# The seam ahead of ret-out, and the first expert's context products

## The reference

```python
y_ret = (jax.nn.silu(g_ret) * o) @ w_ret_o              # o: retention output, normalised per head
y_conv = (cb * u) @ w_conv_o
merged = jax.nn.sigmoid(ga) * y_ret + jax.nn.sigmoid(gb) * y_conv
x = x + g1 * rmsnorm(merged @ w_o)

aff = jax.nn.softmax(hf @ w_router, axis=-1)            # hf: the modulated tokens
vals, idx = lax.top_k(aff.T, cap)                       # cap: 128 for latents, 16 for context
xs = hf[idx]
hid = jax.nn.silu(einsum('ecd,edf->ecf', xs, w_gate)) * einsum('ecd,edf->ecf', xs, w_up)
out = einsum('ecf,efd->ecd', hid, w_down) * vals[..., None]
y = zeros.at[idx].add(out)
```

## Time and profile before

| | us |
|---|---|
| median of 3 runs | 2106.55 |
| lowest, highest | 2105.34, 2106.89 |
| the profiled execution, its time | 2105.37 |
| its span in the profile | 2103.70 |
| PE busy in the span | 1996.7 (95%) |
| DVE busy | 1183.3 (56%) |
| ACT busy | 743.5 (35%) |
| POOL busy | 235.1 (11%) |

### The profile page before, as it was taken

The page is one execution under the profiler, slowest core; times in us unless marked ns, Lnnn a source line. Parts: engine busy times, 40 slices in busy tenths (PEclk is TensorE's granted clock), DMA queues, the critical chain, the costliest instruction groups (busy, mean ns, idle before and its releaser), DMA issues.

```text
span 2103.7 us, 32724 instructions
## 1 busy us (share of the span) xinstructions
PE 1996.7 (95%) x12747; PEld 1727.3 (82%) x12747; DVE 1183.3 (56%) x1623; ACT 743.5 (35%) x840; POOL 235.1 (11%) x241
## 2 busy tenths in 40 slices
PE   6999999989999999999999995799999999999992
PEld 3898988879999999999999884577777777777772
DVE  5654646465554232332122556777777777777765
ACT  7622121231111111111112332455556555556552
POOL 1010101000000000000000123111221111121102
PEclk9999999999999999999999997899999999999996
DMA  9011102224443111112224747388887788888668
GB/s 335 20 46 46 54 32 76 77 60 143 142 139 116 41 34 46 40 50 74 85 85 135 274 145 316 111 322 320 320 308 290 271 321 320 320 308 309 264 254 311
DMA packets 179510, 365.96 MB, mean 174 GB/s; under 512 B 10500, under 2 KB 99532, under 8 KB 178564
## 3 DMA queue, kind: packets, MB, share of 16 engines
q1 hardware_dynamic: 162736, 311.23, 40.6%
q0 software_dynamic: 16624, 54.04, 8.4%
q10 hardware_dynamic: 100, 0.03, 0.0%
HBM read 322.24 MB, written 43.02 MB: 174 GB/s over the span
## 4 chain that ended last, share of the span: by engine, by line
PE 90%; DVE 4%; DMA 4%; issue 1%; SPq 1%; ACT 1%; DVEq 0%; ACTq 0%
PE ps L912 10%; PE ps L913 10%; PE ps L914 10%; PE ps L1175 8%; PE ps L1177 8%; PE ps L1184 8%; PE ps L1193 8%; PE ps L934 3%; PE ps L935 3%; PE ps L936 3%; PE ps L983 2%; PE ps L985 2%; PE ps L984 2%; PE ps L1093 2%; PE ps L1095 1%; PE ps L1094 1%
## 5 line engine op out<-in xcount | busy, mean ns | idle before, releaser
L2080 DVE TENSOR_TENSOR e_lo<-raw,e_hi 128x2048 fp32r<-128x2048 f32 x192 | 439.3, 2290 | 92.8 <-ACT e_hi L1552 92.8
L1552 ACT CAST e_hi<-raw 128x2048 fp32r<-128x2048 f32 x192 | 367.1, 1914 | 213.5 <-PE ps L1184 213.5
L912 PE MATMUL ps<-h_hi,w_hi 128*128 128x384 f32 x960 | 322.1, 335 | 1.0 <-DVE w_lo L1662 1.0
L913 PE MATMUL ps<-h_lo,w_hi 128*128 128x384 f32 x960 | 321.1, 334 | 0.0
L914 PE MATMUL ps<-h_hi,w_lo 128*128 128x384 f32 x960 | 321.0, 334 | 0.0
L1662 DVE TENSOR_TENSOR w_lo<-w_raw,w_hi 128x1024 fp32r<-128x1024 f32 x64 | 78.0, 1219 | 215.3 <-ACT w_hi L1290 215.2
L912 PEld LDWEIGHTS ps<-h_hi,w_hi 128*128 128x128 f32 x960 | 180.6, 188 | 8.9 <-DVE w_lo L1662 4.6
L913 PEld LDWEIGHTS ps<-h_lo,w_hi 128*128 128x128 f32 x960 | 180.5, 188 | 0.0
L914 PEld LDWEIGHTS ps<-h_hi,w_lo 128*128 128x128 f32 x960 | 180.5, 188 | 0.0
L1175 PE MATMUL ps<-e_hi,x_hi 128*128 128x512 f32 x512 | 159.6, 393 | 0.2 <-ACT x_hi L1558 0.2
L1177 PE MATMUL ps<-e_lo,x_hi 128*128 128x512 f32 x512 | 157.7, 389 | 0.0
(11 more groups left out here) (281 smaller groups left out, 3275.6 us busy)
## 6 DMA issues: line engine op xcount, KB each, us to landing
raw<-in_w_gate_dram SPq DMA_DIRECT2D x64, 1024.0 KB, 7.8
raw<-in_w_up_dram SPq DMA_DIRECT2D x64, 1024.0 KB, 14.4
raw<-in_w_down_dram SPq DMA_DIRECT2D x64, 1024.0 KB, 13.0
w_raw<-in_w_in_dram SPq DMA_DIRECT2D x48, 512.0 KB, 4.0
ada_k<-in_w_ada_dram SPq DMA_DIRECT2D x64, 256.0 KB, 2.8
merged_d<-merged POOLq DMA_DIRECT2D x16, 576.0 KB, 3.5
ada<-in_w_ada_dram SPq DMA_DIRECT2D x7, 1024.0 KB, 15.5
ret_part<-merged_d POOLq DMA_DIRECT2D x8, 576.0 KB, 4.0
```

The lines of the kernel that those rows point to most:

```text
L912: pe.matmul(out, w_hi[:, slot, k, :], xh, start=(k == 0), stop=False)
L913: pe.matmul(out, w_hi[:, slot, k, :], xl, start=False, stop=False)
L1552: act.copy(e_hi[u % 4][:].rearrange("p k n -> p (k n)"), raw[(u + 8) % 12][:].rearrange("p k n -> p (k n)"))\
L2080: dve.tensor_tensor(e_lo[u % 4][:].rearrange("p k n -> p (k n)"), raw[(u + 8) % 12][:].rearrange("p k n -> p (k n)"), e_hi[u % 4][:].rearr ...
```

## The change

Two changes are joined.

At the seam, ScalarE splits slot 0 of share 0 after gate 3 and makes `z_hi` 0 to 3 after gate 4, when all outputs are made; slot 1 after gate 5. VectorE's part of slot 0 goes ahead of the fourth normalisation, `z_lo` 0 and 1 ahead of the fifth, `z_lo` 2, 3 and slot 1 between the gatings. TensorE starts the first product of share 0 directly behind the last gate block, and the transposes of the last pair's outputs stand inside it.

At the first expert, the context's selection, its row numbers and its gather come ahead of latent rounds 10 and 11, and its rows are turned on VectorE ahead of round 12. TensorE makes all context products of expert 0 before the latents' rows have come, with 12 and 3 matmuls ahead of them that write what nobody reads. On POOL the context gather is issued ahead of the zero stores, the latent gather behind them and without waiting for their landing. ScalarE waits for that landing ahead of expert 0. SP waits for the first latent gather ahead of the loads of expert 1, and for each load also for `e_lo_done` of the same buffer, since the context product may now be older than the split. The other 15 experts keep their order.

```diff
@@ SP
                 if not first:
                     sp.wait_ge(raw_used, 12 * e - 12 + u + 1)
+                    sp.wait_ge(e_lo_done, 12 * e - 12 + u + 1)
...
+            sp.wait_ge(got_l, 16)
             with sp.Fori(1, EXPERTS) as e:
@@ POOL
             pool.memset(zero[:], 0.0).then_inc(zero_ready, 1)
...
+            pool.wait_ge(h2_stored[0], 16 * 5)
+            pool.wait_ge(sel_read, 1)
+            gather_context(0)
+
             pool.wait_ge(zero_ready, 1)
             with pool.Fori(0, NT) as t:
...
-            pool.wait_ge(ffn_zeroed, 16 * NT + 16)
...
+            pool.wait_ge(sel_read, 4)
+            gather_latents(0)
+            pool.wait_ge(ffn_zeroed, 16 * NT + 16)
@@ PE, seam
-            for g in range(N_G):
-                turn_outputs(PAIRS, g)
+            def first_ret_gate():
+                pe.wait_ge(w_lo_done, T_RETOUT + 1)
+                turns = {(0, 4): (0, 1), (1, 0): (2, 3), (1, 4): (4,)}
+                for b in range(NB):
+                    for k in range(KD):
+                        for g in turns.get((b, k), ()):
+                            turn_outputs(PAIRS, g)
+                        if k == 0:
+                            if b < 2:
+                                pe.wait_ge(gates_out, UNITS * PAIRS - 3 + b)
+                            else:
+                                pe.wait_ge(normed, N_G * PAIRS)
...
+                mm.then_inc(projected, 1)
@@ PE, first expert
+            pe.wait_ge(sel_ready, 1)
+            pe.transpose(ps[0:CAP_C, 3, 128:144], sel_v[0:EXPERTS, CAP_L:CAP], id16)
+            pe.transpose(ps[0:CAP_C, 3, 144:160], sel_f[0:EXPERTS, CAP_L:CAP], id16).then_inc(sel_turned, 1)
+            pe.wait_ge(flip_in, 16)
+            pe.wait_ge(sel_copied, 1)
+            pe.matmul(ps[:, 7, 0:2 * EXPERTS], flip[0:CAP_C, P:2 * P], sel_c[:], start=True, stop=True).then_inc(sel_flipped, 1)
+            keep_busy(3, 12)
+            pe.wait_ge(xc_turned, 1)
+            for u in range(4):
+                first_context(u, 4, 0, xc)
+            for u in range(4, 6):
+                first_context(u, 7, CAP_Q, xc)
+            pe.wait_ge(sel_ready, 2)
...
+            for u in range(6, 8):
+                first_context(u, 7, CAP_Q, xc)
+            pe.wait_ge(sel_read, 3)
+            keep_busy(3, 3)
+            pe.wait_ge(hc_turned, 1)
+            for u in range(8, 12):
+                first_context(u, 7, 0, hcT)
             pe.wait_ge(sel_read, 5)
             turn_rows(0)
-            expert(0, False)
+            expert(0, False, first=True)
@@ ACT
+                    if last and n == 3:
+                        split(T_RETOUT, 2, 0, 0)
+                    if last and n == 4:
+                        act.wait_ge(o_made, N_G * PAIRS)
+                        act.wait_ge(z_in, 16)
+                        for k in range(4):
+                            high_z(k)
                 if last:
-                    split(T_RETOUT, 2, 0, 0)
+                    split(T_RETOUT, 2, 0, 1)
...
+            gate_context(0)
             high_rows(0)
-            expert(0, False)
+            act.wait_ge(ffn_zeroed, 16 * NT + 16)
+            expert(0, False, first=True)
@@ DVE, seam
                 measure(i, 3)
                 if not last:
                     split_panel(i + 1, 3)
+                else:
+                    split(T_RETOUT, 2, 0, 0)
                 normalise(i, 3)
                 measure(i, 4)
                 if last:
-                    split(T_RETOUT, 2, 0, 0)
+                    low_z(0)
+                    low_z(1)
                 normalise(i, 4)
...
-            for g in range(N_G):
-                gate_outputs(PAIRS, g)
...
+            low_z(2)
+            gate_outputs(PAIRS, 0)
+            gate_outputs(PAIRS, 1)
+            low_z(3)
+            gate_outputs(PAIRS, 2)
+            gate_outputs(PAIRS, 3)
+            split(T_RETOUT, 2, 0, 1)
+            gate_outputs(PAIRS, 4)
+            for k in range(4, KD):
...
+                low_z(k)
@@ DVE, selection
             affinities(8)
-            select(*latents, range(10, 12))
             dve.wait_ge(aff_turned, 2)
...
+            dve.tensor_copy(sel_f[0:EXPERTS, CAP_L:CAP], sel_i[0:EXPERTS, CAP_L:CAP]).then_inc(sel_ready, 1)
+            dve.wait_ge(sel_turned, 1)
+            dve.tensor_copy(sel_c[:], ps[0:CAP_C, 3, 128:160]).then_inc(sel_copied, 1)
+            dve.wait_ge(sel_flipped, 1)
...
+            select(*latents, range(10, 12))
+            turn_context(0)
             select(*latents, range(12, CAP_L // 8), ends=True)
...
-            for q in range(3):
-                low(0, q)
+            hidden_context(0, 1)
+            low(0, 0)
+            low(0, 1)
+            low(0, 2)
             low_rows(0)
-            turn_context(0)
             low(0, 3)
-            expert(0, False)
+            expert(0, False, first=True)
```

More of the change, by code:

```diff
@@ L1195, in context, with expert @@
                 mm.then_inc(raw_used, 1)
-            def expert(e, last):
+            def expert(e, last, first=False):
                 for u in range(4):
@@ L1203, in expert @@
                     latent(e, u, 2, x_hi, x_lo)
-                pe.wait_ge(xc_turned, e + 1)
-                for u in range(4):
-                    context(u, 4, 0, xc)
-                pe.wait_ge(out_ready, 2 * e)
-                for u in range(4, 8):
-                    context(u, 7, CAP_Q, xc)
+                if not first:
+                    pe.wait_ge(xc_turned, e + 1)
+                    for u in range(4):
+                        context(u, 4, 0, xc)
+                    pe.wait_ge(out_ready, 2 * e)
+                    for u in range(4, 8):
+                        context(u, 7, CAP_Q, xc)
                 for half in range(2):
-                    pe.wait_ge(hid_done, 3 * e + half + 1)
+                    pe.wait_ge(hid_done, 3 * e + half + (2 if first else 1))
                     for k in range(4 * half, 4 * half + 4):
@@ L1558, in high_rows, with gate_context, expert @@
                     act.copy(x_hi[:, 4 * half:4 * half + 4, :].rearrange("p k n -> p (k n)"), ps[:, 2 + half, :]).then_inc(x_hi_done, 1)
-            def expert(e, last):
+            def gate_context(e):
+                act.wait_ge(raw_used, 12 * e + 4)
+                if not isinstance(e, int) or e:
+                    act.wait_ge(hid_done, 3 * e)
+                act.activation(sg_c[:], ps[:, 4, 0:CAP_Q], ACT.Silu).then_inc(sg_done, 1)
+            def expert(e, last, first=False):
                 for u in range(4, 8):
@@ L1568, in expert @@
                     high(e, u)
-                act.wait_ge(raw_used, 12 * e + 4)
-                act.wait_ge(hid_done, 3 * e)
-                act.activation(sg_c[:], ps[:, 4, 0:CAP_Q], ACT.Silu).then_inc(sg_done, 1)
+                if not first:
+                    gate_context(e)
                 for half in range(2):
@@ L1884, in ret_merge @@
             def ret_merge(n):
-                split(T_RETOUT, 2, n, 1)
+                if not isinstance(n, int):
+                    split(T_RETOUT, 2, n, 1)
                 dve.wait_ge(ada_summed, n)
@@ L2140, in low_rows, with hidden_context, expert @@
                                       x_hi[:, ks, :].rearrange("p k n -> p (k n)").bitcast(F32), ALU.subtract).then_inc(x_lo_done, 1)
-            def turn_context(e):
-                dve.wait_ge(got_c, 16 * (e + 1))
-                dve.transpose(xc[:].rearrange("p k r -> p (k r)"), xg_c[:]).then_inc(xc_turned, 1)
-            def expert(e, last):
+            def hidden_context(e, count):
+                dve.wait_ge(raw_used, 12 * e + 8)
+                dve.wait_ge(sg_done, 3 * e + count)
+                dve.tensor_tensor(hid_c[:], ps[:, 7, CAP_Q:2 * CAP_Q], sg_c[:], ALU.mult).then_inc(hid_done, 1)
+                dve.wait_ge(hid_done, 3 * e + count)
+                dve.transpose(hcT[:].rearrange("p k r -> p (k r)"), hid_c[:]).then_inc(hc_turned, 1)
+            def expert(e, last, first=False):
                 for u in range(4, 11):
@@ L2151, in expert @@
                 for half in range(2):
[L2152 removed]
+                    dve.wait_ge(sg_done, 3 * e + half + (2 if first else 1))
                     hs = hid[:, half * 512:half * 512 + 512]
                     dve.tensor_tensor(hs, ps[:, 2 + half, :], hs, ALU.mult).then_inc(hid_done, 1)
[L2155 to L2159 removed]
+                if not first:
+                    hidden_context(e, 3)
                 for half in range(2):
```

124 lines of the change are left out of this document (62 added, 62 removed).

## The result

| | before | after |
|---|---|---|
| median, us (5 executions each) | 2105.34 | 2092.53 |
| lowest to highest | 2103.44 to 2106.89 | 2091.90 to 2096.56 |
| the profiled execution: time, span | 2105.37, 2103.70 | 2092.53, 2090.8 |

The ratio is 0.9943, 95% interval 0.9932 to 0.9955: 12.0 us less by the ratio, 12.8 by the two profiled executions.

A forecast was written before the change was run, and what follows sets the result against it. TensorE was taken to bound the kernel, so only its idle or low-clock stretches could be won. Seam -5.45 and selection with expert 0 -3.3 (5.3 - 8.6) gave -8.7: median 2106.55 to 2097.8, range 2093.8 to 2103.2.

The forecast's parts named there:

- The seam: Between last head pair and first ret-out share: `ada_acc` chain starts at 448.8, not 454.28, share 1 moving with it; 5.45 less.
- Rival C: At the seam, gating and transposes wait for each other: half the gain, chain only 2.7 earlier; 2100.5, chance 0.12.
- The selection: Selection ahead of expert 0: context chosen and gathered before latent rounds 10 and 11 makes the latent products 5.3 later.
- the first one's price, 6.4: Context gather in the selection: as the program's first indirect transfer, 6.4 us from issue at 1317.7 to landing at 1324.1.
- rival B: In the selection, the context gather issued amid rounds 10 and 11 starts only in VectorE's pause at 1321.9; 2101.9, chance 0.08.
- the 2.2 of waiting on VectorE: In the selection, VectorE waits 2.2 us for the context's rows, since their transposes stand ahead of rounds 12 to 15.
- T': When the last latent index reaches TensorE after the change: forecast at 1333.1, 5.4 later than before.
- the clock's term: At the selection, after TensorE idles 3.2 us, 3.4 us at half clock were assumed.
- Expert 0: First expert loses its context products of 7.04 and 3.59; 5.0 of the first and all of the second won, 8.6 less.
- rival A: In expert 0, the lower clock follows the 1.9 gap ahead of `hid`: sum -7.0, 2099.5, chance 0.14.
- D: At the selection, the context gather is quick and the clock held: -12.1, 2094.4, chance 0.14.
- E: At the selection, zero stores ahead of the latent gather drain slowly and its rows wait: slower, 2112.8, chance 0.04.

The follow-up runs named there:

- seam_only: The kernel before with only the seam's edits (first product of ret-out, `high_z`, `low_z`, order of the splits): 2101.19 us, ratio 0.9975.
- before_quiet: The kernel before with three unread MAX8 passes on VectorE, holding the subtractions back from the first gather: 2107.37 us in one run.
- subtract_beside: The changed kernel with the first `e_lo` subtraction moved ahead of latent rounds 10 and 11, beside the context's gather: 2100.55 us in one run.
- late_context: The changed kernel with four unread MAX8 passes (2.9 us) on VectorE ahead of `turn_context(0)`: 2100.62 us, ratio 0.9972.
- gap_filled: The changed kernel with five unread products in expert 0's gap ahead of the transposes of `hid`: 2092.74 us, ratio 0.9934.
- after_again: The changed kernel measured a second time, with no edit: 2094.34 us, ratio 0.9939.
- held_and_filled: The changed kernel with two unread products in each of two router-stage gaps and five in expert 0's gap ahead of `hid`: 2092.92 us, ratio 0.9935.

## Why the prediction was wrong

**The seam: right.** Forecast 5.45 less at share 1; share 1's products start at 467.90 instead of 473.12, 5.2 less. The `ada_acc` chain was forecast at 448.8 and started at 448.97, the clock was forecast at 1.00 and was. The fifth normalisation, forecast to end at 434.8, started only at 435.29, after a wait of 0.91 for POOL that the forecast did not have; the work behind it took it up. By share 7 it is 6.0 less: the kernel before waited 0.5 each for `w_lo` of shares 1 and 2, the changed one 0.2 once. Rival C (half the gain) is out by seam_only, whose mark at share 0 comes 5.3 earlier.

**The selection: wrong, and this is the step that failed.** "as the first indirect transfer of the program I give it the first one's price, 6.4". The context's gather took 2.8 from issue to landing. The sum had +5.3 here and +1.0 was measured, 4.3 less. The whole forecast missed by 4.1 (12.8 by the two profiles against 8.7); the other errors nearly cancel: expert 0 gave 1.8 less than forecast, the seam 0.5 and the last stage 1.3 more.

Two things were wrong in the 6.4. It was not the price of being first but of the subtraction beside it: before_quiet takes the subtractions away and the price falls to 4.4, subtract_beside puts one beside the context's gather and it rises from 2.8 to 5.0. And it was the price of the other gather: the latents' one brings 128 rows of 1024 numbers, 512 KB, the context's one 128 KB, and with no subtraction beside them they landed in 4.4 to 4.5 and in 2.8. So of the 3.6 that the 6.4 was too high, 2.0 are the subtraction and 1.6 the kind of gather.

The rows were there: the earlier trace rows had a median of 1.0 beside the 3.05, had the context's gather at 3.9 once, and the gather of 3.05 ran from 1331.10, 0.2 behind the start of VectorE's first `e_lo`. I chose between 3.9 and 6.4 by the order in the program, and not by what ran beside each. "No row here shows such a hold" was true of the rows printed and not of the trace, where the context's 16 gathers have a median of 2.17. The section of the Trainium skill that I cited ahead of rival B speaks of this contention too, and I took from it only the two-port modes.

From this one term hang the 2.2 of waiting on VectorE, the idle time of 3.2 on TensorE (1.71 measured) and the clock behind it. T' came 2.9 later and not 5.4; the latents followed 9.3 behind it and not 11.1. late_context, where VectorE comes about as late as forecast (T' 5.7 behind the kernel before), tests the chain behind the term. Its latents come 6.4 later than in the kernel before, where the forecast had 5.3. The clock was at half for some 6.8 us around T' (by the table of its run), where the forecast took 3.4, and the way from T' to the latents is 11.83 and not 11.1. So the chain was right in kind and 1.1 too cheap; the clock's term was mis-sized too, but it never came to bear.

**Expert 0: the path right, 2 us off.** Forecast 8.6 less; up to the start of expert 1 it was 45.44 before (1338.92 to 1384.36) and 38.82 after, 6.6 less. The gap ahead of `hid` was 2.27 instead of 1.9, and rival A, which the sum had put at nothing, took place: the clock fell behind it, at a price of 1.3 (gap_filled) where A had 1.7.

**The end.** 1.3 less in a stage that the change doesn't touch; there after_again had 1.0 less than the kernel before, seam_only the same, held_and_filled 1.0 more. The record doesn't say what sets it; nothing shows it to be a gain of the change.

**The rivals.** D, quick gather and held clock, came nearest: 2094.4 forecast, with the sum -12.1 for -12.0 to -12.8 measured. It was right that the gather is quick and that the clock holds behind T'. That its total fits so well is partly luck: it had 1.9 for the selection (1.0 measured) and 8.6 for expert 0 (6.8), and nothing for the 1.3 of the last stage. B, the gather held up beside VectorE's rounds, is out: 1.08 beside `match_replace` and `max`; what it names does happen, beside another instruction. E is out: the latent gather took 1.01 and landed in 4.5. The estimate of 2.3 for these bytes, worked out from the Trainium skill (DMA: Bandwidth & Descriptors, section Anatomy of one DMA — SWDGE (gpsimd) path), was dismissed with "the trace speaks against it"; 2.8 was measured, and the trace had spoken of something else.

**The range** ended at 2093.8, D's time less 0.6. The two medians of the changed kernel are 2092.53 and 2094.34, so the 1 to 2 us by which the stages that the change doesn't touch differ from profile to profile were not in it; the bound for D should have been some 2 us lower.

## What to carry to other kernels

When one duration of a kind stands out, look at what ran on the other engines in those microseconds before taking it for the price of its place, and look at all instructions of the kind: here 16 others showed the same hold. Take a price from a transfer of the same bytes. Price a delay ahead of TensorE as itself plus the clock that it may cost, and a filling of unread products by the clock it holds. Stages that no edit touches moved by up to 3 us between profiles here, so compare stages by marks, and look at the intervals, before explaining a sum of medians that doesn't close.

## What the runs showed of the hardware

- A gather's issue on POOL takes 0.94 to 1.08 beside `max`, `match_replace` or nothing, 2.53 with a subtraction of two SBUF operands that began 0.7 ahead of it, and 8.02 in one case with three of them back to back. Of 236 gathers issued inside such a subtraction 234 ended 0.82 to 0.95 after a subtraction did; gathers issued 0.3 ahead of one took 1.0. Plain stores issued by POOL inside one took 0.53, as without.
- One subtraction with an operand in PSUM did not hold a gather: at 1338.95 in the kernel before, `x_lo<-ps,x_hi` (128x512) ran beside one of 0.94. It is a quarter as wide, so this is a hint and no test.
- The clock fell behind a gap of 2.27 in seven profiles (0.61 and 0.54 in the changed kernel's) and not in an eighth with the same instructions there (1.00). After 3.10 and 2.68 it was at 0.50, after 1.71 at 1.00; after 1.35 it fell, where 5.61 of idleness stood 8.5 us ahead.
- Sixteen route products took 1.96 to 3.60 at one place, by where the fall of the clock lay; with the gaps beside them filled, 1.96 in three profiles of three.
